# Attention units of two query heads from either key-value head, with scores that alternate between the two halves of the array

## The chip, the cores and the metric

The kernel runs on one core of a Trainium2 chip. The metric is the device time of one execution in microseconds, the median of several. The engines are TensorE (PE, whose weight loads are listed as PEld), VectorE (DVE), ScalarE (ACT), GpSimd (POOL) and SyncE (SP, which issues DMAs). The array of TensorE has 128 rows (the contracted dimension) and 128 columns.

## The reference

A chain of two blocks over 1024 tokens of width 1024, in float32. The part that matters here is the first block's even layer: a sliding-window attention with 8 query heads of 64, which share 2 key-value heads (4 query heads each), blocks of 128 queries, and for each block the keys of the block before it and its own:

```python
q = q.reshape(B, nb, BLOCK, KV_HEADS, GROUP, HEAD_DIM)      # 8 blocks, 2 kv heads, 4 query heads each, 64
kk = jnp.concatenate([jnp.concatenate([kpad, k[:, :-1]], axis=1), k], axis=2)   # 256 keys
scores = jnp.einsum('bnqkgd,bnskd->bnkgqs', q, kk) * (HEAD_DIM ** -0.5)
scores = jnp.where(valid, scores - slopes * dist, NEG)
mx = jnp.maximum(jnp.max(scores, axis=-1, keepdims=True), sink)
p = jnp.exp(scores - mx)
p = p / (jnp.sum(p, axis=-1, keepdims=True) + jnp.exp(sink - mx))
out = jnp.einsum('bnkgqs,bnskd->bnqkgd', p, vv)
...
ya = sliding_window_attention(q, k, v, sinks) * jax.nn.silu(ga)
yb = multiscale_pool(u, pool_w, pool_scale) * jax.nn.silu(gb)
return jnp.concatenate([ya, yb], axis=-1) @ w_out
```

Behind it stand a convolution layer and a second model with its own attention and a large feed-forward part; they take most of the time and the change doesn't touch them.

## The kernel before

Everything is written out by hand, engine by engine: each engine has its own program, in the order of the source, and semaphores join them. There is no scheduler; an engine does its instructions in the order written.

The projections lie transposed in the tile P0, with the width on the 128 partitions: chunks Q0 to Q0+3 hold the queries, K0 the keys, V0 the values, GA0 to GA0+3 the attention's gate, GB0 to GB0+3 the pool's gate. A query chunk Q0+j has query head j of the first key-value head on partitions 0 to 63 and head j of the second on 64 to 127; K0 has the first key-value head's keys on the lower 64 partitions, the second's on the upper.

`block0` is the attention on TensorE. It runs over 16 units t; a unit is one block of 128 queries (n = t // 2) with the four query heads of one key-value head (half = t % 2). For each t the order on TensorE is: `scores` of unit t+1 (four matmuls of 64 rows into `slot(0)`, two PSUM banks, 256 columns for each head), a step of other work (`beside`), `keys_down` of t (transposes of the weights), a second step, `values` of t (matmuls of 64 columns) and `turn` of t-1 (transposes of the output). The steps between are `gate_steps`: the projection of the pool's gate, six matmuls of 512 columns each on all 128 rows; when these have run out, `pool_mix`. In the units of the first block of queries there is no key block before it, so that each head has 128 columns of scores and not 256.

On VectorE, `maxima0` reads the scores, adds the bias (BIAS holds one 128x256 tile for each of the 8 heads), leaves the sums in SS0 and the largest in SMALL, and works out four maxima with the sinks; `output0` scales the values' result, `gate0` multiplies the turned output by its gate. `take_gate` empties a finished gate chunk once in four units. ScalarE copies the transposed weights to SBUF (line 1967) and then takes the next unit's exponentials (`weights0`, line 1952). TensorE waits in `scores` until the maxima of the unit before are done, in `keys_down` for the exponentials, in `values` for the copy, in `turn` for the scaled output.

The weights of the projections come by SP and POOL in a ring of three, and POOL makes the low part of each; a slot comes free when TensorE has finished with it. The projections back to the width (`out0`) start when all units' outputs have been gated.

Of the kernel before, what the change touches and what calls it, by code (L numbers as in the profile page):

```python
# [20 lines left out]
ALU = mybir.AluOpType  # L21
# [7 lines left out]
P = 128  # L29
# [5 lines left out]
HD = 64  # L35
# [173 lines left out]
def build(nc, x, meta, weights, gains, taps, pool_w, pool_scale, conv_w, b_f, sinks, final_g, out):  # L209
    with ExitStack() as ctx:  # L210
# [999 lines left out]
        def _(pe):  # L1210
# [130 lines left out]
            def block0():  # L1341

                pe.wait_ge(evacuated, USE0 + V0 + 1)
                for b in range(NB):
                    m = nc.tensor.transpose(bank(6, 2)[:, b * P:(b + 1) * P], P0[:, V0, b * P:(b + 1) * P], IDENT[:])
                m.then_inc(turned, 1)

                pe.wait_ge(evacuated, USE0 + 14)
                pe.wait_ge(small_in, 16 * 6)
                pe.wait_ge(pooled, 4)  # L1350
                pe.wait_ge(v0_ready, 1)

                def pool_mix(g):
                    if g == 0:
                        pe.wait_ge(evacuated, USE0 + 18)
                    elif g == 1:
                        pe.wait_ge(s0_max, UNITS0)
                    elif g == 2:
                        pe.wait_ge(pool_taken, 1)
                    else:  # L1360
                        pe.wait_ge(pt0_copied, UNITS0)
                    for h in range(2):
                        m = nc.tensor.matmul(mix_bank(g)[:, h * HALF:(h + 1) * HALF], PW[:, g, :],
                                             P0[:, U0 + g, h * HALF:(h + 1) * HALF], start=True, stop=True)
                    m.then_inc(pool_out, 1)

                def gate_steps(n, ks):


                    p = 14 + n  # L1370
                    u = p % NW
                    for k in ks:
                        if k == 0:
                            pe.wait_ge(w_ready, p + 1)
                            pe.wait_ge(evacuated, USE0 + p)
                        m = three(slot(1), WH[:, u, k * P:(k + 1) * P], WL[:, u, k * P:(k + 1) * P], XH[:, k, :], XL[:, k, :],
                                  k == 0, k == KD - 1)
                        if k == KD - 1:
                            m.then_inc(psum_full, 1)

                def beside(t, part):


                    n = 2 + 2 * t + part
                    if n < 4 * KD:
                        gate_steps(n // KD, (n % KD,))
                    else:
                        pool_mix(n - 4 * KD)

                def scores(t):  # L1390
                    n, half = divmod(t, 2)
                    r = half * HD
                    if t >= 1:
                        pe.wait_ge(s0_max, t)
                    k0 = P if n == 0 else 0
                    for j in range(GROUP):
                        m = nc.tensor.matmul(slot(0)[:, j * 2 * P + k0:(j + 1) * 2 * P],
                                             P0[r:r + HD, Q0 + j, n * P:(n + 1) * P],
                                             P0[r:r + HD, K0, (n - 1) * P + k0:(n + 1) * P],
                                             start=True, stop=True)  # L1400
                    m.then_inc(s0_ready, 1)

                def keys_down(t):

                    pe.wait_ge(p0_ready, t + 1)
                    if t >= 1:
                        pe.wait_ge(pt0_copied, t)
                    first = 1 if t < 2 else 0
                    for j in range(GROUP):
                        for h in range(first, 2):  # L1410
                            m = nc.tensor.transpose(bank(4, 2)[:, (2 * j + h) * P:(2 * j + h + 1) * P],
                                                    SS0[:, t % 2, j, h * P:(h + 1) * P], IDENT[:])
                    m.then_inc(pt0_ready, 1)

                def values(t):
                    n, half = divmod(t, 2)
                    first = 1 if n == 0 else 0
                    pe.wait_ge(pt0_copied, t + 1)
                    if t >= 1:
                        pe.wait_ge(yt0_ready, t)  # L1420
                    for j in range(GROUP):
                        for h in range(first, 2):
                            m = nc.tensor.matmul(bank(6)[:, j * HD:(j + 1) * HD], PT0[:, 2 * j + h, :],
                                                 VT0[:, n - 1 + h, half * HD:(half + 1) * HD],
                                                 start=h == first, stop=h == 1)
                    m.then_inc(o0_ready, 1)

                def turn(t):
                    pe.wait_ge(yt0_ready, t + 1)
                    if t >= 1:  # L1430
                        pe.wait_ge(ya_ready, t)
                    for m_ in range(2):
                        m = nc.tensor.transpose(bank(7)[:, m_ * P:(m_ + 1) * P], YT0[:, t % 2, m_ * P:(m_ + 1) * P],
                                                IDENT[:])
                    m.then_inc(ya_turned, 1)


                scores(0)
                gate_steps(0, (0, 1))
                for t in range(UNITS0):  # L1440
                    if t + 1 < UNITS0:
                        scores(t + 1)
                    beside(t, 0)
                    keys_down(t)
                    beside(t, 1)
                    values(t)
                    if t >= 1:
                        turn(t - 1)
                turn(UNITS0 - 1)
                pool_mix(2)  # L1450
                pool_mix(3)
# [1014 lines left out]
        def _(dve):  # L2466
# [112 lines left out]
                                       op0=ALU.mult, op1=ALU.mult).then_inc(pool_taken, 1)  # L2579

            def maxima0(t):
                n, half = divmod(t, 2)
                dve.wait_ge(s0_ready, t + 1)
                if t >= 2:
                    dve.wait_ge(pt0_ready, t - 1)
                if t >= 1:
                    dve.wait_ge(s0_max, t)
                k0 = P if n == 0 else 0
                mx = SMALL[:, 48:52]
                for j in range(GROUP):  # L2590
                    ins = v.tensor_tensor_reduce(SS0[:, t % 2, j, k0:], slot(0)[:, j * 2 * P + k0:(j + 1) * 2 * P],
                                                 BIAS[:, half * GROUP + j, k0:], QK_SCALE, -3e38, ALU.add, ALU.max,
                                                 SMALL[:, 48 + j:49 + j])
                then(ins)
                sinks_ = SINKS[:, half * GROUP:(half + 1) * GROUP]
                then(v.tensor_tensor(mx, mx, sinks_, ALU.max))
                then(v.tensor_scalar(SMALL[:, 8 * (t % 2):8 * (t % 2) + 4], mx, -1.0, None, ALU.mult))
                v.tensor_tensor(SMALL[:, 32 + 4 * (t % 4):36 + 4 * (t % 4)], sinks_, mx,
                                ALU.subtract).then_inc(s0_max, 1)

            def output0(t):
                n, half = divmod(t, 2)
                dve.wait_ge(p0_ready, t + 1)
                if t >= 1:
                    dve.wait_ge(yt0_ready, t)
                den = SMALL[:, 52:56]
                then(v.tensor_tensor(den, SMALL[:, 16 + 4 * (t % 4):20 + 4 * (t % 4)],
                                     SMALL[:, 32 + 4 * (t % 4):36 + 4 * (t % 4)], ALU.add))
                then(v.reciprocal(SMALL[:, 56:60], den))
                dve.wait_ge(o0_ready, t + 1)  # L2610
                if t >= 2:
                    dve.wait_ge(ya_turned, t - 1)
                for j in range(GROUP):
                    ins = v.tensor_scalar(YT0[:, t % 2, j * HD:(j + 1) * HD], bank(6)[:, j * HD:(j + 1) * HD],
                                          SMALL[:, 56 + j:57 + j], None, ALU.mult)
                ins.then_inc(yt0_ready, 1)

            def gate0(t):
                n, half = divmod(t, 2)
                dve.wait_ge(ya_turned, t + 1)  # L2620
                if t == 0:
                    dve.wait_ge(gate_done, 4)
                ga = P0[:, GA0 + 2 * half:GA0 + 2 * half + 2, n * P:(n + 1) * P]
                v.tensor_tensor(ga, bank(7)[:, 0:2 * P].rearrange("p (a b) -> p a b", a=2), ga,
                                ALU.mult).then_inc(ya_ready, 1)

# [739 lines left out]
```

## Time and profile before

| | |
|---|---|
| median of 3 runs | 2125.38 us (2124.88 to 2126.38) |
| span of the profiled execution | 2125.7 us |
| PE busy | 2043.9 us, 96% of the span |
| DVE, POOL, ACT busy | 1332.1 us (63%), 1093.3 us (51%), 686.0 us (32%) |
| the 16 attention units | about 187.6 to 313.7 us of the span |

The profiled execution's span lies 0.3 us above the median of the runs, inside their spread. Busy times are sums of an engine's records; matmuls are pipelined, so a record reaches over the start of the next one, and what a matmul takes of the queue is read from start to start. "Idle before" is the time that an engine stood still ahead of an instruction, with the work that ended it. In the timeline, records of one kind that stand next to each other are merged into one row, with their count.

### The profile page before, as it was taken

To read this page: it belongs to the slowest core of one execution; us is meant where nothing else is said; L and a number is where in the kernel's file an instruction comes from. 1 tells how busy PE (TensorE), PEld (TensorE's weight loads), DVE (VectorE), ACT (ScalarE), POOL (GpSimd) and SP (SyncE) were. 2 spreads that over 40 slices of the span, in tenths; PEclk is the share of its full clock that TensorE was granted. 3 is DMA by queue.
4 is the path that set the end of the run, shared out by engine and by line. 5 is a ranking of instruction groups with operands and counts; after the bars stand their busy time and mean duration, and the time that the engine had idled before them with its cause. 6 is when DMAs were issued, how large, how long until landed. Compare 5 with 4: busy or idle time off the path is not lost.

```text
span 2125.7 us, 25085 instructions
## 1 busy us (share of the span) xinstructions
PE 2043.9 (96%) x9336; PEld 1602.8 (75%) x9336; DVE 1332.1 (63%) x1847; ACT 686.0 (32%) x1146; POOL 1093.3 (51%) x932
## 2 busy tenths in 40 slices
PE   7999999999999999899999899999999999999997
PEld 6887877777776767787788555677788887888886
DVE  6136553679998898442264467656744446777769
ACT  3002553331125331321021254423322323554542
POOL 3221014567684884344324300025876787888885
PEclk9999999999999999899999999999999999999999
DMA  5431116544454543346523443235556767666652
GB/s 184 139 119 61 39 40 242 174 163 138 159 183 134 178 139 99 119 160 194 181 80 106 116 102 74 95 129 169 192 191 215 233 214 279 215 241 230 218 178 109
DMA packets 103352, 331.24 MB, mean 156 GB/s; under 512 B 12544, under 2 KB 12800, under 8 KB 102464
## 3 DMA queue, kind: packets, MB, share of 16 engines
q1 hardware_dynamic: 55040, 190.64, 28.0%
q0 software_dynamic: 29808, 104.35, 14.2%
q10 hardware_dynamic: 18384, 34.66, 4.4%
q8 instruction: 75, 1.23, 0.2%
q14 instruction: 45, 0.37, 0.1%
HBM read 268.55 MB, written 46.20 MB: 148 GB/s over the span
## 4 chain that ended last, share of the span: by engine, by line
PE 54%; issue 27%; POOL 11%; DVE 6%; ACT 1%; DMA 1%; POOLq 0%; DVEq 0%; ACTq 0%
PE PS L1228 37%; PE PS L1782 13%; POOL WL L980 5%; DVE PS L2704 3%; PE PS L1482 3%; POOL WH L973 1%; DMA WH<-weights 1%; POOL VSL L1183 1%; DVE ACC L3222 1%; DVE ACC L3243 0%; DVE OT L3297 0%; POOL WL L1178 0%; PE PS L1337 0%; PE PS L1691 0%; POOL WSL L1090 0%
## 5 line engine op out<-in xcount | busy, mean ns | idle before, releaser
L1228 PE MATMUL PS<-XHM,WH 128*128 128x512 f32 (+1 forms) x1464 | 527.9, 388 | 22.2 <-DVE XLM L2480 12.0
L1228 PE MATMUL PS<-XLM,WH 128*128 128x512 f32 (+1 forms) x1464 | 512.9, 378 | 0.0
L1228 PE MATMUL PS<-XHM,WL 128*128 128x512 f32 (+1 forms) x1464 | 510.8, 376 | 0.0
L973 POOL DMA_DIRECT2D WH<-weights x145 | 83.6, 577 | 819.0 <-PE PS L1228 797.6
L980 POOL TENSOR_TENSOR WL<-WRAW,WH 128x1024 fp32r<-128x1024 f32 x145 | 352.3, 2430 | 25.6 <-DMA WH<-weights 22.6
L1228 PEld LDWEIGHTS PS<-XHM,WH 128*128 128x128 f32 x1464 | 272.1, 191 | 93.2 <-issue 19.1
L1228 PEld LDWEIGHTS PS<-XLM,WH 128*128 128x128 f32 x1464 | 279.0, 191 | 56.3 <-issue 3.1
L1228 PEld LDWEIGHTS PS<-XHM,WL 128*128 128x128 f32 x1464 | 278.7, 190 | 52.6
L2704 DVE SCALAR_TENSOR_TENSOR PS<-G,TAPW,PS 128x512 f32<-128x512 f32 x348 | 262.7, 755 | 11.7
L3222 DVE TENSOR_TENSOR ACC<-ACC,PS 128x1024 f32<-128x1024 f32 (+1 forms) x113 | 119.8, 1073 | 19.3 <-PE PS L1228 17.0
L1228 PE MATMUL PS<-OPH,VSH 128*128 128x512 f32 x256 | 100.9, 394 | 2.2 <-issue 2.2
L1228 PE MATMUL PS<-OPH,VSL 128*128 128x512 f32 x256 | 100.6, 393 | 0.0
L1228 PE MATMUL PS<-OPL,VSH 128*128 128x512 f32 x256 | 100.5, 393 | 0.0
L3202 DVE TENSOR_TENSOR OPL<-PS,OPH 128x512 fp32r<-128x512 f32 x98 | 67.6, 690 | 46.2 <-ACT PS L2406 45.7
L1649 PE MATMUL PS<-PT,VX 128*128 128x512 f32 (+4 forms) x224 | 87.7, 494 | 5.1 <-ACT PT L2267 5.1
L1183 POOL TENSOR_TENSOR VSL<-VS,VSH 128x512 fp32r<-128x512 f32 x64 | 85.3, 1353 | 2.9 <-ACT VSH L2413 2.9
L1035 POOL TENSOR_TENSOR RBM<-RBM,SQH 128x512 f32<-128x512 f32 x58 | 74.9, 1291 | 23.1 <-ACT SQH L2027 21.8
L2489 DVE TENSOR_TENSOR PS<-PS,SQH 128x512 f32<-128x512 f32 x60 | 41.6, 695 | 65.4 <-ACT SQH L1914 64.5
L1228 PE MATMUL PS<-OPH,WH 128*128 128x512 f32 x192 | 75.6, 394 | 1.5 <-DVE OPL L3198 0.8
L1228 PE MATMUL PS<-OPL,WH 128*128 128x512 f32 x192 | 75.3, 392 | 0.0
L1228 PE MATMUL PS<-OPH,WL 128*128 128x512 f32 x192 | 75.1, 391 | 0.0
L2406 ACT COPY PS<-OPR 128x512 f32<-128x512 f32 x98 | 57.4, 585 | 53.4 <-DVE OPL L3202 53.4
(377 smaller groups left out, 3952.3 us busy)
## 6 DMA issues: line engine op xcount, KB each, us to landing
WRAW<-weights SPq DMA_DIRECT2D x207, 512.0 KB, 3.5
WH<-weights POOLq DMA_DIRECT2D x191, 512.0 KB, 4.6
OPR<-inner SPq DMA_DIRECT2D x56, 512.0 KB, 6.4
inner<-STAGE ACTq DMA_DIRECT2D x56, 256.0 KB, 4.5
inner<-TOUT ACTq DMA_DIRECT2D x48, 256.0 KB, 4.7
XTOK<-x SPq DMA_DIRECT2D x8, 512.0 KB, 7.3
x_kept<-X SPq DMA_DIRECT2D x4, 1024.0 KB, 7.3
X<-x_kept SPq DMA_DIRECT2D x8, 512.0 KB, 4.9
```

Of the source, the lines that this page charges most:

```text
L973: g.dma_start(WH[:, u, :], weights[WORDER[p]]).then_inc(w_hi[u], 16)
L980: g.tensor_tensor(WL[:, u, :], WRAW[:, u, :], WH[:, u, :].bitcast(F32), ALU.subtract)\
L1035: g.tensor_tensor(dst, SSUMH[1], SQH[:, 1, i % 2, :], ALU.add).then_inc(tap_added, 1)
L1183: g.tensor_tensor(VSL[e][:, two], VS[e][:, two], VSH[e][:, two].bitcast(F32), ALU.subtract).then_inc(w_ready, 1)
L1228: m = nc.tensor.matmul(dst[:, a:b], w, v[:, a:b], start=first and n == 0, stop=last and n == 2)
L1482: m = nc.tensor.matmul(bank(6), diagonal(b, i - TAP_BATCH[part]), G1[:, c, h * HALF + j:(h + 1) * HALF + j], start=i == 0, stop=i == TAPS - 1,
L1649: m = nc.tensor.matmul(o[:, q0 - half * HALF:q0 - half * HALF + w], VX[0:keys, j, c, HD * e:HD * e + P], PT2[n % 3][0:keys, a:a + w], star ...
L1782: m = nc.tensor.matmul(dst, a[:, c], b[:, k, :], start=new and k == 0 and i == 0, stop=k == 3 and i == 2, skip_group_check=True)
L2406: nc.scalar.copy(bank(LOW_BANK), OPR[x][:, a, :]).then_inc(a_hi, 1)
L2704: then(v.scalar_tensor_tensor(out=acc, in0=src, scalar=tap, in1=acc, op0=ALU.mult, op1=ALU.add))
L3202: v.tensor_tensor(OPL[x][:, a, :], bank(LOW_BANK), OPH[x][:, a, :].bitcast(F32), ALU.subtract).then_inc(a_split, 1)
L3222: v.tensor_tensor(dst, dst, src, ALU.add).then_inc(evacuated, 1)
```

## The change

A unit is still one block of queries with four heads, and there are still 16. It now has two heads of either key-value head: with m = t % 2, the heads 2m and 2m+1 of the first and of the second. In `scores` the four matmuls take the lower 64 rows, the upper, the lower, the upper. The lower heads' scores go to the first of the two banks of slot 0, the upper ones' to the second. Values, bias rows, sinks and gate chunks are chosen to fit.

```diff
                 def scores(t):
-                    n, half = divmod(t, 2)
-                    r = half * HD
+                    n, m_ = divmod(t, 2)
                     if t >= 1:
                         pe.wait_ge(s0_max, t)
                     k0 = P if n == 0 else 0
-                    for j in range(GROUP):
-                        m = nc.tensor.matmul(slot(0)[:, j * 2 * P + k0:(j + 1) * 2 * P],
-                                             P0[r:r + HD, Q0 + j, n * P:(n + 1) * P],
-                                             P0[r:r + HD, K0, (n - 1) * P + k0:(n + 1) * P],
-                                             start=True, stop=True)
+                    for j in range(2):
+                        for half in range(2):
+                            r, i = half * HD, 2 * half + j
+                            m = nc.tensor.matmul(slot(0)[:, i * 2 * P + k0:(i + 1) * 2 * P],
+                                                 P0[r:r + HD, Q0 + 2 * m_ + j, n * P:(n + 1) * P],
+                                                 P0[r:r + HD, K0, (n - 1) * P + k0:(n + 1) * P],
+                                                 start=True, stop=True)
...
                 def values(t):
-                                                 VT0[:, n - 1 + h, half * HD:(half + 1) * HD],
+                                                 VT0[:, n - 1 + h, j // 2 * HD:(j // 2 + 1) * HD],
...
             def maxima0(t):
-                                                 BIAS[:, half * GROUP + j, k0:], QK_SCALE, -3e38, ALU.add, ALU.max,
+                                                 BIAS[:, j // 2 * GROUP + 2 * m + j % 2, k0:], QK_SCALE, -3e38, ALU.add, ALU.max,
                                                  SMALL[:, 48 + j:49 + j])
                 then(ins)
-                sinks_ = SINKS[:, half * GROUP:(half + 1) * GROUP]
+                sinks_ = SINKS[:].rearrange("p (a b c) -> p a b c", a=2, b=2)[:, :, m, :]
+                mx = mx.rearrange("p (a c) -> p a c", a=2)
                 then(v.tensor_tensor(mx, mx, sinks_, ALU.max))
...
             def gate0(t):
-                ga = P0[:, GA0 + 2 * half:GA0 + 2 * half + 2, n * P:(n + 1) * P]
+                ga = P0[:, GA0 + m:GA0 + m + 3:2, n * P:(n + 1) * P]
```

No instruction moves to another place on its engine. This is TensorE's program around one unit before (PS the PSUM, P the tile P0, XHM, XLM, WH and WL the high and low parts of the gate's operands; the first row is the scores):

```order
L1397 MATMUL PS<-P_76 128x256 x4
L1228 MATMUL PS<-XHM,WH 128x512 x2
L1228 MATMUL PS<-XLM,WH 128x512 x2
L1228 MATMUL PS<-XHM,WL 128x512 x2
L1411 MATMUL PS<-IDENT,SS_81 128x128 x8
```

And the same place in the changed program:

```order
L1398 MATMUL PS<-P_76 128x256 x4
L1228 MATMUL PS<-XHM,WH 128x512 x2
L1228 MATMUL PS<-XLM,WH 128x512 x2
L1228 MATMUL PS<-XHM,WL 128x512 x2
L1412 MATMUL PS<-IDENT,SS_81 128x128 x8
```

Rows, counts and sizes are the same; the line of the scores is one further down, and the half of the array that each of the four uses, which these rows don't name, is what differs.

## Rows read from the trace of the kernel before

**Rows 1.** The page, busy time of each engine (us, share of the span, instructions).
```profile
PE 2043.9 (96%) x9336; PEld 1602.8 (75%) x9336; DVE 1332.1 (63%) x1847; ACT 686.0 (32%) x1146; POOL 1093.3 (51%) x932
```

**Rows 2.** Table by stretch: start:end and length, busy time (instructions), clock, DMA share, GB/s.
```profile
186.00:187.60 1.60, 0.00 (x0) 0.03 (x1) 1.60 (x3) 1.22 (x2) 1.60 (x1) 1.00 0.96 289
...
190.00:192.00 2.00, 2.00 (x6) 1.60 (x5) 1.83 (x13) 0.00 (x0) 0.00 (x0) 0.50 0.00 0
...
202.00:313.00 111.00, 109.90 (x653) 90.40 (x651) 60.18 (x258) 57.38 (x155) 11.76 (x8) 1.00 0.11 39
```

**Rows 3.** Waits, 187 to 320 us: who for whom, us in total, times, longest.
```profile
ACT PT L1967 <- PE PS L1411: 51.5, 14, 4.7
...
PE PS L1397 <- DVE VT L2563: 1.7, 1, 1.7
...
PE PS L1433 <- DVE P L2624: 1.2, 1, 1.2
...
PE PS L1363 <- DVE P L2578: 0.7, 1, 0.7
```

**Rows 4.** Timeline of PE over one unit: start, length of all, merged records.
```profile
228.16 1.99 PE L1397 MATMUL PS<-P 64*128 64x256 f32 x8
230.08 0.74 PE L1228 MATMUL PS<-XHM,WH 128*128 128x512 f32 x2
...
231.58 1.03 PE L1411 MATMUL PS<-IDENT,SS 128*128 128x128 f32 x8
...
233.85 1.89 PE L1423 MATMUL PS<-VT,PT 128*128 128x64 f32 x16
...
235.90 0.48 PE L1397 MATMUL PS<-P 64*128 64x256 f32 x1
```

**Rows 5.** Timeline, PE's last scores record of that unit, and PEld (weight loads) around it.
```profile
229.78 0.38 PE L1397 MATMUL PS<-P 64*128 64x256 f32 x1
...
225.98 1.89 PEld L1423 LDWEIGHTS PS<-VT,PT 128*128 128x128 f32 x16
...
228.16 1.59 PEld L1397 LDWEIGHTS PS<-P 64*128 64x128 f32 x8 [0.17 <-issue]
...
230.08 0.30 PEld L1228 LDWEIGHTS PS<-XHM,WH 128*128 128x128 f32 x2 [0.33 <-issue]
```

**Rows 6.** Groups by form, PE, 187.5 to 313.7 us: the scores' records.
```profile
L1397 PE MATMUL PS<-P 64*128 64x256 f32 x112 | 27.9, 389 | 0.0
...
L1397 PE MATMUL PS<-P 64*128 64x128 f32 x16 | 2.3, 283 | 1.7 <-DVE VT L2563 1.7
```

**Rows 7.** Timeline of PE, the scores of the second unit and the next gate step.
```profile
193.20 1.16 PE L1397 MATMUL PS<-P 64*128 64x128 f32 x8
...
194.28 0.73 PE L1228 MATMUL PS<-XHM,WH 128*128 128x512 f32 x2
```

**Rows 8.** Timeline of DVE, a plain unit and one that takes a gate.
```profile
228.88 0.42 DVE L2624 TENSOR_TENSOR P<-PS,P 128x256 f32<-128x256 f32 x1
230.19 0.42 DVE L2591 CUSTOM_DVE_ANT_0 SS<-PS,BIAS 128x256 f32<-128x256 f32 x1 [0.90 <-PE PS L1397]
...
232.09 0.16 DVE L2598 TENSOR_TENSOR SMALL<-SINKS,SMALL 128x4 f32<-128x4 f32 x1
...
242.94 2.11 DVE L2607 TENSOR_TENSOR SMALL<-SMALL 128x4 f32<-128x4 f32 x1
...
246.40 0.41 DVE L2591 CUSTOM_DVE_ANT_0 SS<-PS,BIAS 128x256 f32<-128x256 f32 x1
```

**Rows 9.** Timeline: ACT after a change of table, and PE's transposes two units later.
```profile
229.23 0.19 ACT L1956 ACTIVATE SMALL<-SMALL 128x4 f32<-128x4 f32 x1
232.66 1.01 ACT L1967 COPY PT<-PS 128x1024 f32<-128x1024 f32 x1 [3.24 <-PE PS L1411]
...
247.06 1.04 PE L1411 MATMUL PS<-IDENT,SS 128*128 128x128 f32 x8
```

**Rows 10.** Timeline of PE behind the last unit.
```profile
313.11 0.41 PE L1433 MATMUL PS<-IDENT,YT 128*128 128x128 f32 x2 [1.21 <-DVE P L2624]
```

More of the change, by code:

```diff
@@ L1415, in values @@
                 def values(t):
-                    n, half = divmod(t, 2)
+                    n = t // 2
                     first = 1 if n == 0 else 0
@@ L2581, in maxima0 @@
             def maxima0(t):
-                n, half = divmod(t, 2)
+                n, m = divmod(t, 2)
                 dve.wait_ge(s0_ready, t + 1)
@@ L2591, in maxima0 @@
                     ins = v.tensor_tensor_reduce(SS0[:, t % 2, j, k0:], slot(0)[:, j * 2 * P + k0:(j + 1) * 2 * P],
-                                                 BIAS[:, half * GROUP + j, k0:], QK_SCALE, -3e38, ALU.add, ALU.max,
+                                                 BIAS[:, j // 2 * GROUP + 2 * m + j % 2, k0:], QK_SCALE, -3e38, ALU.add, ALU.max,
                                                  SMALL[:, 48 + j:49 + j])
                 then(ins)
-                sinks_ = SINKS[:, half * GROUP:(half + 1) * GROUP]
+                sinks_ = SINKS[:].rearrange("p (a b c) -> p a b c", a=2, b=2)[:, :, m, :]
+                mx = mx.rearrange("p (a c) -> p a c", a=2)
                 then(v.tensor_tensor(mx, mx, sinks_, ALU.max))
-                then(v.tensor_scalar(SMALL[:, 8 * (t % 2):8 * (t % 2) + 4], mx, -1.0, None, ALU.mult))
-                v.tensor_tensor(SMALL[:, 32 + 4 * (t % 4):36 + 4 * (t % 4)], sinks_, mx,
+                then(v.tensor_scalar(SMALL[:, 8 * (t % 2):8 * (t % 2) + 4], SMALL[:, 48:52], -1.0, None, ALU.mult))
+                v.tensor_tensor(SMALL[:, 32 + 4 * (t % 4):36 + 4 * (t % 4)].rearrange("p (a c) -> p a c", a=2), sinks_, mx,
                                 ALU.subtract).then_inc(s0_max, 1)
             def output0(t):
-                n, half = divmod(t, 2)
                 dve.wait_ge(p0_ready, t + 1)
@@ L2618, in gate0 @@
             def gate0(t):
-                n, half = divmod(t, 2)
+                n, m = divmod(t, 2)
                 dve.wait_ge(ya_turned, t + 1)
```

## The prediction

> **What bounds the kernel now.** I read the page first: TensorE is busy 96% of the span [rows 1], so the question is whether the first block's attention is one of the stretches where it has no slack. The table by stretch says so: from 202 to 313 us, fourteen of the sixteen units and the end of the last, PE is busy 109.9 of 111.0 us at a granted clock of 1.00 [rows 2]. The waits of PE from 187 to 320 us, where one would see the softmax chain holding it up, are three: 1.7 us before the first scores, 1.2 and 0.7 us behind the last unit [rows 3]. Between, PE waits for nobody, and the longest wait inside the units, 51.5 us of ACT's, is a wait for PE [rows 3]. So a unit costs what PE's queue costs: 235.90 − 228.16 = 7.74 us from one unit's scores to the next unit's [rows 4].
>
> Then I read that queue. The scores hold it from 228.16 to 230.08, 1.92 us of the 7.74; the rest is two gate steps, transposes, values and the turn, which the change leaves alone [rows 4]. The scores' four matmuls are eight records of 64 rows [rows 4]: a float32 matmul runs as two passes, each with its own weight load. The records are alike, so that the two passes of one matmul stand next to each other is an assumption. From 1.99 us for eight records, of which the first lasts 0.48 and the last 0.38 [rows 4, 5], the starts lie (1.99 − 0.48)/7 = 0.216 us apart. A load takes about 0.10 us: by that the first record, whose load nothing covers, exceeds the others; sixteen loads of the values in 1.89 us give 0.12 at most [rows 5]. Inside the scores, loads are therefore hidden behind the pass before, and the price is passes alone. Ahead of the first load lies 0.17 us in which the weight side does nothing, and 0.33 us behind the last [rows 5].
>
> **The change part by part.** The instructions on every engine stay the same in number and place. What changes is which 64 rows a matmul uses. Before, all four matmuls of a unit lie on the same half of the array, one behind the other. Now lower and upper alternate, and their results go to different banks: the two lower heads to the first 512 columns of slot 0, the two upper ones to the second.
>
> *Scores, units 2 to 15.* No row of before shows two matmuls on different halves next to each other, so the price is bounded from both sides. Call the matmuls A (lower), B (upper), C (lower), D (upper), with passes A1 A2 B1 B2 and so on. If a pass starts as soon as its own half is free and the one ahead of it in the queue has started, then A2 waits for A1; B1 runs beside A2; B2 waits for B1, C1 runs beside B2; C2 waits, D1 beside it; D2. That is five pass lengths instead of eight, 3 × 0.216 = 0.65 us less. At the other end nothing overlaps and the saving is nothing, or every change of half costs something (rivals). I take five: the halves hold separate weights, read separate rows and write separate banks, and eight loads of 0.10 us fit into five passes (0.8 in 1.08 us), so nothing else in the rows keeps them apart. 112 records of 256 columns [rows 6] are 14 units: 14 × 0.65 = 9.1 us.
>
> The Trainium skill speaks of this price twice. In "TensorE: Matmul & The Clock Gate", Part 3, it says that a weight load overlaps running matmuls only where the row group differs. Rows 4 and 5 disagree: at 0.216 us from pass to pass on one half, the load is hidden already. By that rule eight passes would have cost 8 × (0.216 + 0.10) = 2.5 us, not 1.92, and the alternation would also have brought those loads, an estimated 0.2 us a unit more; the sum goes by the rows.
>
> *Scores, units 0 and 1.* With one key block a pass is half as long: eight records of 128 columns take 194.28 − 193.20 = 1.08 us [rows 7], 0.84 less than 1.92, so a pass is about 0.11 us and no longer than a load. If loads run one behind the other they become the bound here; I count nothing, and 2 × 3 × 0.11 = 0.7 us at best.
>
> *DVE.* The maxima read another bias row per head, and two four-element operations read their sinks through a two-by-two pattern; the gate multiplies chunks two apart in place of neighbours. Counts and sizes are as they were: nothing, and all of it stands beside PE. If a unit's DVE work grew it would be covered up to the gap before its maxima, 0.90 us [rows 8], of which 0.25 is left once the scores end 0.65 us earlier.
>
> *What is late next.* VectorE: after the gate multiply (228.88 + 0.42 = 229.30) the maxima wait until 230.19 for the scores; they would start at about 229.54 and still wait for PE. In the four units that take a gate, a small operation like the one of 2.11 us shown puts the maxima off, there to 246.40 [rows 8]; scores 0.65 us earlier leave that start where it is, so the sums of that unit end at about 248.5 (246.40 + 2.1, from 230.19 to 232.09 + 0.16). ScalarE's copy of the transposed scores, which comes before its exponentials, starts 1.08 us after the transposes start and lasts 1.01 [rows 4, 9]; with transposes at 247.06 in that unit [rows 9], it ends at 249.1, in the new kernel at 248.5. Just in time, and no loss: the exponentials end 2.2 us later, at 250.7, and the transposes that read them, before one unit on at 247.06 + 7.74 = 254.8, would start at 253.5. ScalarE in its longest unit, with the change of table, is done at 229.23 + 0.19 = 229.42, and the transposes that need it start at 231.58 [rows 4, 9]: 2.2 us of slack, 1.5 afterwards. The copy itself and the values behind it both follow the transposes, and nothing between them is shortened.
>
> *Behind the stage.* After the last unit PE waits 1.21 us for a DVE multiply [rows 10]; that chain hangs on the last values and moves as a whole. Weights, kept x and the second half's loads are released by PE's steps or the last gate, so they move too. I let the whole gain through.
>
> *The clock.* PE stands still from 186.0 to 187.6 us and has a granted clock of 0.50 (1.2 GHz) from 190 to 192 [rows 2]. This lies at the first units, and shorter scores may lengthen or shorten it a little. I take 1.5 us either way, the spread of the runs (2124.88 to 2126.38), and nothing in the sum.
>
> **The sum.** The profiled span of 2125.7 us stands for the median 2125.38. 2125.38 − 9.1 = **2116.3 us** (2114 to 2118 for this case alone).
>
> **The rivals.**
> *The halves keep better pace: four pass lengths.* If B1 could start beside A1, or the passes stand A1 B1 A2 B2, a unit saves 4 × 0.216 = 0.86 us: 12.1 us, 2113.3, and with the short units near 2112.5. For it: nothing in the rows ties B1 to A2. Against it: A2 stands ahead of B1 in PE's queue, and no row shows a matmul that starts ahead of an earlier one. The skill's page on TensorE, Part 3, gives a pack of tiles one matmul's length plus 4 ns for each further tile, which would be this case, though it also has matmuls in strict order, which is five lengths. 8 in 100.
>
> *The load comes late.* If a half's load leaves the queue only when the matmul ahead of it has started, it shows at each change of half: each saves 0.216 − 0.10 to 0.12 us. 3 × 14 × 0.10 to 0.116 = 4.2 to 4.9 us, 2120.5 to 2121.2, say 2120.9. For it: the idle 0.17 us ahead of the first load shows that PE doesn't always fetch ahead [rows 5]. Against it: inside the scores it does. 16 in 100.
>
> *No overlap.* Float32 passes run one at a time whatever rows they use: the change doesn't do what it says, 2125.4. For it: no row of this kernel shows two of them side by side; a record reaches over the next start by some 0.16 us (0.38 against 0.216) everywhere. 14 in 100.
>
> *Each change of half drains the array.* The entry into the 64-row scores costs 0.17 us of standstill and an exposed load of 0.10 [rows 5]. If a change of half costs the same, three of them in 16 units are 48 × 0.10 to 0.27 = 4.8 to 13.0 us: 2130.2 to 2138.4, slower. It decides as soon as the loss at a change exceeds the pass that it hides (0.216 us), or at once if nothing is hidden. For it: exactly this is seen at the entry. Against it: that entry changes from 128 rows to 64, while here the shape stays and only the half moves. The skill ("TensorEngine Tiling (Array Packing)", Key Properties) has the drain at a change of tiling mode and not of tile; the 0.17 us agrees with its first half, and no run shows the second. 12 in 100.
>
> **How the numbers follow.** Forecast 50, four lengths 8, late load 16, no overlap 14, drain 12 in 100. The range from 2113.0 to 2126.0 holds the forecast, half of the four lengths, the late load and nearly all of no overlap: a little over 8 in 10; left out are the drain and the far side of the best case. A difference under 0.2% (4.25 us, so 2121.1 to 2129.6) can't be told from none here. Faster: 50 + 8 + half of the late load, 66; the same: 8 + 14 = 22; slower: 12.
>
> **What would show it.** The scores' time from first record to the next gate step should be 1.27 us in place of 1.92, a unit 7.1 in place of 7.74, PE's waits in the stage still those three. In the records, upper-half passes should start while a lower-half pass runs. If the scores still take 1.92 us, there is no overlap; 1.6 is the late load, 1.06 four lengths, over 2.1 the drain. If the scores shrink and the unit doesn't, my reading of PE as the only bound is wrong, and a DVE or ACT row will stand among PE's waits.

## The result and the profile after

The changed kernel took 2110.12 us (median of 4, 2108.63 to 2115.88) against 2125.88 for the kernel before in the same comparison: a ratio of 0.9934, 95% interval 0.9919 to 0.995. It is faster, as forecast, but by more than the forecast of 2116.3 and beyond the range's lower end of 2113.0. In the medians that is 15.8 us. Two further comparisons of the same kernel (below) gave 0.9940 and 0.9941, 12.6 us of 2125 by these ratios (11.5 and 12.6 in their medians); I take 12.6 as the size of the gain, and the other 3 us of the first comparison as what executions differ by.

PE's timeline over a unit, the answer to [rows 4] (start, length of all, merged records):

```profile
223.78 1.14 PE L1398 MATMUL PS<-P 64*128 64x256 f32 x8
224.84 0.73 PE L1228 MATMUL PS<-XHM,WH 128*128 128x512 f32 x2
...
226.34 1.03 PE L1412 MATMUL PS<-IDENT,SS 128*128 128x128 f32 x8
...
228.15 0.62 PE L1228 MATMUL PS<-XHM,WL 128*128 128x512 f32 x2
228.61 1.89 PE L1424 MATMUL PS<-VT,PT 128*128 128x64 f32 x16
230.34 0.39 PE L1434 MATMUL PS<-IDENT,YT 128*128 128x128 f32 x2
230.65 1.14 PE L1398 MATMUL PS<-P 64*128 64x256 f32 x8
```

From the scores to the next gate step it is 224.84 − 223.78 = 1.06 us instead of 1.92; the unit is 230.65 − 223.78 = 6.87 us instead of 7.74. Nothing else in the unit changed its length. 1.06 is the number that the prediction put down for four pass lengths. Cut into short windows, the same eight passes show how (matmuls first, then loads; a row names the records that touch the window, so the counts grow from window to window):

```profile
223.78 0.49 PE L1398 MATMUL PS<-P 64*128 64x256 f32 x2
223.78 0.70 PE L1398 MATMUL PS<-P 64*128 64x256 f32 x4
224.53 0.38 PE L1398 MATMUL PS<-P 64*128 64x256 f32 x2
...
223.78 0.19 PEld L1398 LDWEIGHTS PS<-P 64*128 64x128 f32 x2 [0.17 <-issue]
223.88 0.19 PEld L1398 LDWEIGHTS PS<-P 64*128 64x128 f32 x2
```

Two passes fill 0.49 us together, where one filled 0.48 before [rows 4]: they start at nearly the same time. The next two end 0.21 us after them (0.70 less 0.49), one pass length, and the last two run to the end side by side. The loads do the same: two begin at 223.78 and lie within 0.19 us, about the length of one, and the next two begin 0.10 us later. So loads of different halves don't follow each other, and the short units gain as well:

```profile
192.67 0.71 PE L1398 MATMUL PS<-P 64*128 64x128 f32 x8
193.32 0.73 PE L1228 MATMUL PS<-XHM,WH 128*128 128x512 f32 x2
```

0.65 us, where [rows 7] gave 1.08. The sum of both: 14 × 0.86 + 2 × 0.43 = 12.9 us. The trace agrees. The last of the pool's matmuls behind the units started at 319.0 us before and at 306.0 now, 13.0 earlier, of which 0.1 was there at the first scores already (187.60 before, 187.49 now):

```profile
L1363 PE MATMUL PS<-P,PW x16: 592/595/1057, 305.5 to 319.0; 128*128 128x512 f32 x16
```

```profile
L1363 PE MATMUL PS<-P,PW x16: 592/592/1219, 292.5 to 306.0; 128*128 128x512 f32 x16
```

(The first is the kernel before, the second the changed one: shortest, median and longest in ns, first and last start.) PE's waits up to 315 us are those of [rows 3] and one new one, for VectorE, where the output projection begins; by it some 0.6 us of the gain is lost again:

```profile
PE PS L1398 <- DVE VT L2564: 1.7, 1, 1.7
PE PS L1434 <- DVE P L2625: 1.2, 1, 1.2
PE PS L1363 <- DVE P L2579: 0.7, 1, 0.7
PE PS L1228 <- DVE XLM L2481: 0.6, 1, 0.6
```

The span fell by more than the stage, from 2125.7 to 2107.9 us, 17.8. The other 4.8 us, on balance, lie behind this attention, in stretches with the same work on PE. The widest of them begins where the second block's attention waits for its keys (kernel before, then changed kernel; stretch and length, busy time of PE, PEld, DVE, ACT and POOL, granted clock, DMA share, GB/s):

```profile
1196.00:1262.00 66.00, 54.78 (x240) 34.69 (x239) 34.48 (x51) 30.12 (x48) 12.06 (x17) 0.90 0.51 111
```

```profile
1182.10:1244.60 62.50, 51.86 (x240) 32.90 (x239) 34.44 (x51) 30.14 (x48) 12.09 (x17) 0.95 0.53 117
```

240 matmul records in both, 3.5 us apart, with a mean granted clock of 0.90 and 0.95. Some 0.6 us of that is PE's wait for the keys themselves, a DMA; the rest is PE's own work, 54.78 us against 51.86:

```profile
1206.48 0.77 PE L1627 MATMUL PS<-QQ,KK 128*128 128x512 f32 x1 [5.19 <-DMA KK<-KL]
...
1192.01 0.76 PE L1628 MATMUL PS<-QQ,KK 128*128 128x512 f32 x1 [4.59 <-DMA KK<-KL]
```

```profile
1208.00:1212.00 4.00, 4.00 (x14) 2.49 (x14) 0.00 (x0) 0.93 (x2) 2.18 (x1) 0.50 1.05 245
...
1194.10:1198.10 4.00, 4.00 (x19) 2.73 (x18) 0.00 (x0) 1.15 (x3) 2.21 (x1) 0.83 0.98 229
```

(In both fences the kernel before stands first.) Two microseconds after the wait the granted clock is still 0.50 in the one execution, its lower level (1.2 GHz), and 0.83 on average in the other: after a wait of PE the clock stayed low for longer in the one than in the other. Whether that belongs to the change is what the second to fourth experiments ask.

### The profile page after: what moved, and what is told of

It is laid out like the page before. It is cut to its first block, busy times and chain, and to the rows that moved or that the text cites. A ratio compares the mean times of both kernels' runs of the same rounds, so it can differ in the third digit from the quotient of the medians.

```text
span 2107.9 us, 25085 instructions
## 1 busy us (share of the span) xinstructions
PE 2027.6 (96%) x9336; PEld 1588.8 (75%) x9336; DVE 1330.8 (63%) x1847; ACT 686.4 (33%) x1146; POOL 1093.6 (52%) x932
## 4 chain that ended last, share of the span: by engine, by line
PE 54%; issue 27%; POOL 11%; DVE 6%; ACT 1%; DMA 1%; POOLq 0%; DVEq 0%; ACTq 0%
PE PS L1228 37%; PE PS L1783 13%; POOL WL L980 5%; DVE PS L2705 3%; PE PS L1483 3%; POOL WH L973 1%; DMA WH<-weights 1%; DVE ACC L3223 1%; POOL VSL L1183 1%; DVE ACC L3244 1%; DVE OT L3298 0%; POOL WL L1178 0%; PE PS L1337 0%; PE PS L1692 0%; POOL WSL L1090 0%
```

## The experiments

**1. Does the order matter?** The forecast rested on passes that start in program order. This run keeps the new units and puts the two lower matmuls ahead of the two upper ones.

```diff
-                    for j in range(2):
-                        for half in range(2):
+                    for half in range(2):
+                        for j in range(2):
                             r, i = half * HD, 2 * half + j
```

> The changed kernel with its units of two heads from either key-value head, but the four matmuls of the scores in the order lower, lower, upper, upper. Theory 'each half has its own line': a pass starts when its own half is free, even if an earlier matmul in TensorE's program still waits for the other half. Then the order is indifferent: scores 1.06 us from first record to the next gate step, the attention stage as short as in the changed kernel, total 2110 us (2108 to 2114). Rival 'passes start in program order, and the passes of neighbours of different halves pair up': only the second lower and the first upper matmul stand next to each other, one to two of eight pass lengths overlap: scores 1.5 to 1.7 us, 3 to 6 us faster than the kernel before, 2119 to 2122 us. If regrouping the heads had a gain of its own on VectorE or ScalarE, the total would lie below what the scores' time gives.

2110.74 us (2108.94 to 2111.45), ratio 0.9936 (0.9924 to 0.9949). Its unit in PE's timeline, and its first two passes in a short window:

```profile
222.48 1.14 PE L1398 MATMUL PS<-P 64*128 64x256 f32 x8
223.56 0.73 PE L1228 MATMUL PS<-XHM,WH 128*128 128x512 f32 x2
...
222.48 0.49 PE L1398 MATMUL PS<-P 64*128 64x256 f32 x2
```

1.08 us: the alternation itself is worth at most 0.02 us a unit. What counts is that a unit has two matmuls for either half. Two passes again fill 0.49 us from the start: the upper half takes up its first pass although four passes for the lower half, one running and three waiting, stand ahead of it. The rival, starts in program order, is out, and with it the five lengths of the forecast. What lets the later pass go first, the array's queue or an order that the program is given below the level read here, these records don't tell.

**2. Is the gain given back when the passes are?** The scores of every unit are computed twice.

```diff
+                    for again in range(2):
                     for j in range(2):
                         for half in range(2):
```

(the loop's body one level further in)

> The changed kernel with every unit's scores computed twice, in the same alternating order, the second writing the same values. Eight more passes a unit in four pass lengths: scores 1.06 + 0.86 = 1.92 us, as in the kernel before; the attention stage ends as late as before, 12.9 us later than in the changed kernel. Theory 'the rest of the gain is when the later stages begin' (waits of TensorE at which the granted clock falls, of a length that differs from one execution to another): total 2125.5 us (2122 to 2128), the whole 15.8 us given back. Rival 'the new units also help elsewhere': 2110.1 + 12.9 = 2123.0 us or less, with the later stages as short as in the changed kernel in every execution. Third: doubling the passes needs more than four lengths, scores 2.0 us or more, total above 2128.

2123.58 us (2120.17 to 2126.61) against 2123.89 for the kernel before in the same comparison, ratio 0.9998 (0.9989 to 1.0007). The unit:

```profile
226.60 2.00 PE L1399 MATMUL PS<-P 64*128 64x256 f32 x16
228.53 0.74 PE L1228 MATMUL PS<-XHM,WH 128*128 128x512 f32 x2
```

Sixteen passes in 1.93 us, the time that eight took before. With the scores back at their old length nothing is left of the gain: the new grouping of heads brings and costs nothing elsewhere that this comparison could see (0.2%). In microseconds the run lay near the rival's 2123.0, but the kernel before did too; the ratio decides.

**3. Half of it.** The scores are computed twice in the odd units alone (`for again in range(1 + m_)`).

> The changed kernel with the scores computed twice in the odd units alone: seven units of 0.86 us and one of 0.43 us, 6.5 us more on TensorE. Theory 'the rest is when the later stages begin': the attention stage ends 6.5 us later than in the changed kernel; the total is 2116.6 us with up to 3 us either way, since the later stages begin at yet another time and their low-clock stretches fall otherwise. Rival 'a fixed gain elsewhere': 2116.6 us within 1 us and the later stages as in the changed kernel.

2117.39 us (2115.04 to 2119.74), ratio 0.9967 (0.9956 to 0.9978): in the medians 2123.89 − 2117.39 = 6.5 us faster than before, where 12.9 − 6.5 = 6.4 was due. The last pool matmul starts at 312.8 us, 6.8 behind the changed kernel's. Against the kernel before, this comparison's medians give gains of 0.3, 6.5 and 11.5 us for scores twice, twice in the odd units and once (the run below), where 0, 6.4 and 12.9 were due: time on PE in this stage goes through to the end, as closely as the executions let one see. The median lies within 1 us of 2116.6, as the rival wanted; the executions spread over 4.7 us, as the theory wanted. This run doesn't tell those two apart.

**4. The same kernel again**, in two comparisons.

> The changed kernel once more beside the others on this chip, for the spread. Both theories: scores 1.06 us, attention stage 12.9 us shorter than before, total 2110 us (2108 to 2116). If the later gain of some 3 us comes from low-clock stretches it should differ between executions by a few us, and this profile's later stages need not agree with the first profile's.

> The changed kernel on the same chip as the run with the values split by columns: 2108 to 2113 us, attention stage about 13 us shorter than before, and the later stages again other than in the earlier profiles by up to 4 us.

2112.42 us (ratio 0.9940, 0.9928 to 0.9953) and 2112.47 us (0.9941, 0.9928 to 0.9954). In both the last pool matmul starts at nearly the same time as in the first profile, 305.7 and 306.4 us, but their spans are 2111.7 and 2111.8 us, not 2107.9. The stretch of the second block's attention in the first of them:

```profile
1181.70:1247.60 65.90, 54.71 (x239) 34.68 (x238) 34.44 (x50) 30.20 (x48) 12.08 (x17) 0.90 0.51 111
```

65.9 us at 0.90, as in the kernel before, in the changed kernel itself. So the 3.5 us belong to the execution and not to the change. What in an execution decides how long the clock stays low after a wait stays open.

**5. How far ahead does the idle half find its work?** The scores twice again, now with all four lower matmuls (eight passes) ahead of the four upper ones.

```diff
-                    for j in range(2):
-                        for half in range(2):
+                    for half in range(2):
+                        for j in (0, 1, 0, 1):
```

> The changed kernel with the scores computed twice, the four lower matmuls (eight passes) all ahead of the four upper ones. How far ahead does the array's idle half find its work? If the upper half's passes start beside the lower ones however many stand ahead, the scores take 1.92 us as in the run with alternating order twice, and the total is about 2123.5 us (2120 to 2127). If the look ahead ends after a few passes, the upper half starts late: with the four passes that the run in the order lower, lower, upper, upper has shown, four of sixteen passes stay alone on either side, 12 lengths in place of 8: 0.2 + 12 x 0.216 = 2.8 us, 14 units of 0.86 us and two of 0.43 more, 2136 us.

2139.0 us (2135.0 to 2143.32), ratio 1.0065 (1.0045 to 1.0085), where the same passes in alternating order gave 0.9998.

```profile
224.79 2.96 PE L1398 MATMUL PS<-P 64*128 64x256 f32 x16
227.69 0.74 PE L1228 MATMUL PS<-XHM,WH 128*128 128x512 f32 x2
...
225.33 0.59 PE L1398 MATMUL PS<-P 64*128 64x256 f32 x2
225.76 0.49 PE L1398 MATMUL PS<-P 64*128 64x256 f32 x2
225.98 0.70 PE L1398 MATMUL PS<-P 64*128 64x256 f32 x4
226.41 0.49 PE L1398 MATMUL PS<-P 64*128 64x256 f32 x2
226.73 0.38 PE L1398 MATMUL PS<-P 64*128 64x256 f32 x1
```

2.90 us in place of 1.93. Up to about 225.7 the passes go singly (two records in 0.59 us are one behind the other), from 225.76 on two at a time (two in 0.49, four in 0.70, two in 0.49), and from 226.73 singly again. So four lower passes run alone at the start and four upper ones at the end, twelve lengths for eight, as the second case of the expectation had it; its 2136 us was 3 short. The time is 2.90 − 1.93 = 0.97 us longer: four lengths are 0.86, and the other 0.11 is about one load (0.10). The halves don't have queues of their own without limit. The first upper pass starts beside the fifth lower one: three lower passes wait ahead of it then, as in experiment 1. One pass earlier there were four, and it didn't start. So alternating is the safe order, though at two matmuls for each half it makes no difference.

**6. The same by columns.** If halves of the rows work side by side, loads included, halves of the columns may. The values are sixteen passes of 64 columns, each as long as its load of 128. This run splits each weight tile into its first and last 64 columns, whose results go to the lower and the upper 64 partitions.

```diff
-                            m = nc.tensor.matmul(bank(6)[:, j * HD:(j + 1) * HD], PT0[:, 2 * j + h, :],
+                            for c in range(2):
+                                q = slice(c * HD, (c + 1) * HD)
+                                m = nc.tensor.matmul(bank(6)[q, j * HD:(j + 1) * HD], PT0[:, 2 * j + h, q],
```

> The changed kernel with the values' matmuls split by columns as the scores are split by rows: each weight tile of 128 columns goes in as two of 64, for the queries 0 to 63 and 64 to 127, with the results on the two halves of the partitions. Twice as many instructions, each with half a load. Theory 'the halves of the array work side by side, also by columns, loads included': the values, bound by sixteen loads of about 0.11 us, fall from 1.73 to about 0.9 us a unit and the stage by some 11 us: 2100 us (2096 to 2104), faster than the changed kernel. Rival 'loads of two column halves follow each other': the same 1.73 us and a little for the change of shape: 2110 to 2116. Second rival 'each of the 32 instructions keeps its own floor of time': values 2 us or more and the stage longer, over 2118.

2104.68 us (2103.69 to 2108.02), ratio 0.9907 (0.9889 to 0.9925), the fastest kernel of this study, and just above the range expected. Beside the changed kernel in one comparison:

> The changed kernel with the values' weight tiles split by columns, once more, beside the changed kernel on the same chip. If its gain is the shorter values alone (7 us or more from the stage), it stays ahead of the changed kernel by 7 to 11 us in the medians: 2100 to 2106 us against 2108 to 2113. If the first timing owed it to low-clock stretches that fell well, the two lie within 4 us.

2103.56 us (2102.87 to 2107.69; 0.9908, 0.9893 to 0.9923) against 2112.47: 8.9 us less. In the profiles of these two the last pool matmul starts at 297.5 and 306.4 us, and the first scores at 186.80 and 187.77, so some 8 us of it lie in the stage. PE's timeline of the first of the two runs, and the loads of the values:

```profile
224.80 0.63 PE L1228 MATMUL PS<-XHM,WL 128*128 128x512 f32 x2
225.36 1.15 PE L1426 MATMUL PS<-VT,PT 128*64 128x64 f32 x32
226.45 0.44 PE L1436 MATMUL PS<-IDENT,YT 128*128 128x128 f32 x2
226.81 1.14 PE L1398 MATMUL PS<-P 64*128 64x256 f32 x8
...
233.19 1.13 PE L1398 MATMUL PS<-P 64*128 64x256 f32 x8
...
225.36 1.01 PEld L1426 LDWEIGHTS PS<-VT,PT 128*64 128x64 f32 x32 [0.37 <-ACT PT L1970]
...
225.36 0.14 PEld L1426 LDWEIGHTS PS<-VT,PT 128*64 128x64 f32 x2 [0.37 <-ACT PT L1970]
225.36 0.20 PEld L1426 LDWEIGHTS PS<-VT,PT 128*64 128x64 f32 x4 [0.37 <-ACT PT L1970]
```

32 passes in 226.45 − 225.36 = 1.09 us, where sixteen of twice the load took 1.73 (235.58, where the turn began before, less 233.85 of [rows 4]). The unit is 6.38 us, 0.49 shorter and not the 0.83 that was expected. The values give 0.64 of it. From the start of the last matmuls ahead of them to the values it is 225.36 − 224.80 = 0.56 us in place of 228.61 − 228.15 = 0.46, and the turn lasts 226.81 − 226.45 = 0.36 in place of 230.65 − 230.34 = 0.31: that takes 0.15 back. The loss ahead of the values comes with the entry into the new shape: 0.37 us without a load ahead of the first. The row puts them down to ScalarE's copy, and that has the smaller share of them: the copy ran from 224.07 us for 1.01, to 225.08.

```profile
224.07 1.01 ACT L1970 COPY PT<-PS 128x1024 f32<-128x1024 f32 x1 [1.88 <-PE PS L1412]
```

How much of the rest is the change of shape and how much the end of the step ahead wasn't measured. The loads of the column halves do run together: two that begin at 225.36 lie within 0.14 us, the next two end 0.06 us after them, and so 32 take 1.01 us, 0.03 each, less than half a load of 128 columns (0.10).

## Why the prediction was right in sign and short in size

- *What bounds the stage* was right. PE's queue alone sets the unit: what the scores lost in length the unit lost (0.86 of 0.87 us), and experiments 2 and 3 give it back in proportion, as closely as the executions let one see. One reading on the way was wrong without harm: the longest wait in [rows 3]'s window was not ACT's 51.5 us but POOL's 106.8, which is for PE as well (kernel before):

```profile
POOL WH L973 <- PE PS L1228: 106.8, 4, 28.0
```

- *The step that failed* is "a pass starts as soon as its own half is free and the one ahead of it in the queue has started". The second condition doesn't hold. A pass of the other half starts beside the first one even with three more waiting ahead of it (experiment 1), so the eight passes take four lengths and not five. That is one pass length a unit, 14 × 0.216 = 3.0 us.
- *The short units* were counted at nothing, because loads were taken to follow each other. Loads of the two halves run together, and the two units gave 2 × 0.43 = 0.9 us. Together 9.1 + 3.0 + 0.9 = 13.0, against 12.9 measured at the end of the stage. Behind it the prediction let the whole gain through; the new wait there takes some 0.6 us, so that 12.3 are left, against 12.6 in the later comparisons.
- *The rival with four lengths* had this mechanism's time, 2112.5 to 2113.3 us, against 2112.4 in the later comparisons; it got 8 in 100 because the order of the queue was taken for a law of starts. No row of the kernel before could show it: there, no two neighbours could have overtaken each other.
- *The clock* was allowed 1.5 us either way at the attention's own wait. The executions differ by more, and at other places: 3.5 us in the one stretch shown, most of it by the clock. The lower end of 2113.0 left out half of the four-length case and all of this. That the first comparison came out at 2110.12, below even the four lengths, is the luck of executions and no part of the mechanism.
- *DVE* was right as off the path and nearer to it than said: of the 0.90 us ahead of the maxima [rows 8] nothing is left in the unit shown, where 0.25 was forecast; the maxima now follow the gate multiply within 0.05 us. Their waits for scores fell from 12.1 us in twelve units to 1.3 us in one (kernel before, then changed kernel; behind them the changed kernel's unit):

```profile
DVE SS L2591 <- PE PS L1397: 12.1, 12, 2.1
DVE SS L2592 <- PE PS L1398: 1.3, 1, 1.3
...
224.50 0.41 DVE L2625 TENSOR_TENSOR P<-PS,P 128x256 f32<-128x256 f32 x1
224.96 0.42 DVE L2592 CUSTOM_DVE_ANT_0 SS<-PS,BIAS 128x256 f32<-128x256 f32 x1
```

- *The Trainium skill.* "TensorE: Matmul & The Clock Gate", Part 3, gives a pack of tiles one matmul's length plus 4 ns for each further tile; the pairs here fill 0.49 us against 0.48 for one, which agrees, though in pairs of passes. The same part has matmuls in strict order of program from start to end; experiments 1 and 5 fit that only if the order was changed before the array saw it. The drain at a change of tiling mode and not of tile ("TensorEngine Tiling (Array Packing)", Key Properties) agrees: 0.17 us ahead of the scores as before, and 0.216 us from pair to pair inside.

## What to carry to other kernels

Matmuls with a contraction of 64 that stand next to each other cost about half (here 1.06 us in place of 1.92) when half of them lie on the upper 64 rows, loads included, with the results in different banks as here (the same bank for both halves wasn't tried). Choose what a unit of work is so that both halves have work within a few matmuls of each other; strict alternation matters only when a row of one half grows long. Where PE's queue is the bound and its passes are as long as their loads, a split by columns is worth a try as well.

## What had not been expected of the hardware

- A pass for the second half begins beside the first half's running one over three waiting passes of that half, and not over four (experiments 1 and 5).
- Two weight loads of different row halves take about the time of one (0.19 us for both records, each 0.18 to 0.19 long).
- A column split takes sixteen passes that are as long as their loads from 1.73 us to 1.09; loads of the two column halves run together (two within 0.14 us).
- The same kernel's profiles differ by 3.4 us in one stretch with the same work (62.5 and 65.9 us, granted clock 0.95 and 0.90).
